# Input tiles of SyncE's queue wait for weight loads of GpSimd's queue

## The chip, the cores and the metric

The kernel runs on the eight cores of one Trainium2 chip, one program on all of them. Each core has five engines that run their own instruction streams: TensorE (PE, with its weight loads as PEld), VectorE (DVE), ScalarE (ACT), GpSimd (POOL) and SyncE (SP). Sixteen DMA engines move data between the memory of the chip and the core's own memory. Here two engines issue DMAs: SyncE asks for input tiles and writes the output (queue q1 of the profile), GpSimd asks for weights, which are float32 in memory and bfloat16 on arrival (queue q0). The metric is the device time in microseconds of the slowest core; less is better.

## The reference, cut to what matters

One layer of a decoder trunk over x of (4, 4096, 1024):

```python
h = rmsnorm(x, norm_mix)
proj = h @ w_in                       # 4608 columns: u_pool, u_rnn, u_gate, two merge gates
y_pool = pool_mixer(u_pool, w_pool_grp, pool_scale) @ w_pool_out   # causal means over 2/4/8/16
v = causal_depthwise_conv(u_rnn, conv_w, conv_b)                   # width 4
hr = rg_lru(v, ...)                   # h_t = a_t h_{t-1} + b_t, a sequential scan over time
y_rnn = (hr * gelu(u_gate)) @ w_rnn_out
x = x + (g_merge[0] * y_pool + g_merge[1] * y_rnn) @ w_o
h = rmsnorm(x, norm_ffn)
x = x + (silu(h @ w_ffn_gate) * (h @ w_ffn_up)) @ w_ffn_out        # inner width 2816
return rmsnorm(x, norm_final)
```

## The kernel before

Each of the four sequences is shared by two cores. An even core (role a) computes the first 2240 positions, an odd core (role b) the rest. Role b has no state from its neighbour: it first runs a shortened pass over the first 2240 positions in five tiles ("prefix") to get the scan's state, and then its own positions. Both roles are in one program; behind a common head each engine loads the role (L1242) and branches (L1246).

All data are held transposed, channels on partitions and time along the free axis, in tiles of 256 to 512 columns. An input tile of w columns is four buffers `xt` of two channel blocks each, and one DMA per buffer (`load_tile`). For the first norm ScalarE squares a buffer (L623), GpSimd adds the squares up (L638, L640) or TensorE sums them directly, TensorE sums over partitions (L667), ScalarE makes the reciprocal root (L671, L674), and VectorE makes `h` (L682). TensorE then runs the projections, eight matmuls for each weight tile and column tile (L705). In the recurrent branch a group of eight matmuls `bank<-h,wu` is followed by the convolution (ScalarE L745, VectorE L757), a cast to `vb` (L765, on GpSimd), two gate matmuls (L770) and their tanh (L780).

Nothing of the order is written by hand. `Graph` records the operations with their buffers; `Planner.run` places them on the five engines by keys and a cost model, in which one DMA follows the other at `dma_rate` (185,000 bytes per us) with `dma_lat` (2.2 us) behind; `place` and `reuse` give the buffers addresses. Only then `signals` turns dependences into semaphore waits. Each engine executes its list in order, so whatever waits holds up all that stands behind it. Every operation has a planned `start` and `end`. For a DMA, `end` is the planned landing.

Besides true dependences `signals` adds one kind of wait on purpose: a weight load on GpSimd, outside the head, waits for the last input tile whose planned landing is not after the load's planned start. Input tiles wait for no weight.

The head (the same in both roles) asks for the first tile of 260 columns and the constants on SyncE, and on GpSimd for `wu` (the first of four), `keep_rg` and the other three `wu`. Behind the branch role b's SyncE asks for sixteen buffers in a row, those of prefix tiles two to five, and role a's for eight, those of its tiles two and three. GpSimd goes on with weights, five in role b and some twenty in role a before it runs dry.

Of the kernel before, what the change touches and what calls it, by code (L numbers as in the profile page):

```python
# [142 lines left out]
class Planner:  # L143
# [273 lines left out]
    def signals(self, dma_count):  # L417

        seq = sorted(self.g.ops, key=lambda o: (o.start, o.idx))
        pos = {}  # L420
        for e in ENGINES:
            for i, o in enumerate(self.order[e]):
                pos[o.idx] = i
        chan_last = {}
        for e in ("sp", "pool"):
            n = 0
            for o in self.order[e]:
                if not o.nbytes:
                    continue
                c = (e, n % DMA_SEMS[e])  # L430
                o.sem = c
                o.val = 16 * (n // DMA_SEMS[e] + 1)
                p = chan_last.get(c)
                if p is not None:
                    o.deps.append(p)
                chan_last[c] = o
                n += 1

        tiles = sorted([o for o in self.order["sp"] if o.nbytes and o.tag != "out"], key=lambda o: o.end)
        for o in self.order["pool"][sum(h.eng == "pool" for h in self.head):]:  # L440
            if o.nbytes:
                t = [x for x in tiles if x.end <= o.start]
                if t:
                    o.deps.append(t[-1])
        for o in self.head:
            o.sig = not o.nbytes
        for o in seq:
            for d in o.deps:
                if d.nbytes or d.eng != o.eng or o.eng != "pe":
                    d.sig = True  # L450
        for e in ENGINES:
            v = 0
            for o in self.order[e]:
                if o.nbytes:
                    continue
                if o.sig:
                    v += 1
                    o.sem = e
                    o.val = v
        know = {e: {} for e in ENGINES}  # L460
        self.waits = {}
        for o in seq:
            k = know[o.eng]
            need = {}
            for d in sorted(o.deps, key=lambda d: -d.start):
                if not d.nbytes and d.eng == o.eng == "pe":
                    continue
                if k.get(d.sem, 0) >= d.val or need.get(d.sem, (0,))[0] >= d.val:
                    continue
                need[d.sem] = (d.val, d)  # L470
            out = []
            for s, (v, d) in sorted(need.items(), key=lambda x: -x[1][1].end):
                if k.get(s, 0) >= v:
                    continue
                out.append((s, v))
                k[s] = v
                for ks, kv in d.know.items():
                    if k.get(ks, 0) < kv:
                        k[ks] = kv
            self.waits[o.idx] = out  # L480
            o.know = dict(k)
            if o.sem is not None:
                o.know[o.sem] = max(o.know.get(o.sem, 0), o.val)
        self.chan_last = chan_last
# [11 lines left out]
class Role:  # L496
# [464 lines left out]
    def chunk(self, ci, widths, kk, pre, wus, col):  # L961
# [153 lines left out]
        begin=dict(pe=6.0, act=4.0, dve=3.0, pool=9.0, sp=9.5), window=72.67, table_pen=78.88, dma_rate=185000.0, dma_lat=2.2,  # L1115
# [17 lines left out]
        begin=dict(pe=14.0, act=9.0, dve=11.5, pool=15.0, sp=10.0), window=94.49, table_pen=12.12, dma_rate=185000.0,  # L1133
        dma_lat=2.2, lag=0.08, pe_lag=0.5, bank_lag=0.05, lead=16.65, xlead=8.05, reserve=16380.0, near=29.3, cap=191092.0,
# [198 lines left out]
```

How the kernel before makes its waits and increments, by code:

```python
        def emit(e, name, pl, lo=0, hi=None):  # L1225
            for o in pl.order[name][lo:hi]:
                for s, v in pl.waits[o.idx]:
                    e.wait_ge(sems[s], v)
                ins = o.fn(e)
                if o.nbytes:
                    ins.then_inc(sems[o.sem], 16)
                elif o.sig:
                    ins.then_inc(sems[name], 1)
            if name == "sp" and hi is None:
                for o in pl.role.out_ops:
                    e.wait_ge(sems[o.sem], o.val)
```

## Time and profile before

| | before |
|---|---|
| median of 3 runs (lowest to highest) | 1023.6 us (1023.18 to 1025.88) |
| the profiled execution's own time | 1024.35 us |
| its longest span (core 3, role b) | 1022.8 us |
| its shortest span (core 2, role a) | 1016.8 us |
| TensorE busy, core 3 | 924.4 us (90%) |
| VectorE, ScalarE, GpSimd busy | 591.4, 556.7, 336.8 us |
| wait of TensorE on DMA wu | 11.0 us, in two pieces |

A span runs from the first to the last instruction of one core. The time is about that of the longest span with what lies around it, here 1.55 us in the profiled execution. The profile is of one execution; all cores' traces were read. The engines' busy times are shares of the same span and overlap; an idle engine costs time only where another waits for it.

### The profile page before, as it was taken

The page shows a single profiled execution, that of the slowest core. Times are in us where ns is not written, and L with a number is a line of the kernel's source. Part 1 is how long each engine was busy: PE and PEld are TensorE (multiplying, and loading weights), DVE is VectorE, ACT ScalarE, POOL GpSimd, SP SyncE. Part 2 cuts the span into 40 slices and gives each one's busy share as a digit, 9 for nine tenths or more (in the row PEclk, how much of TensorE's full clock was granted, in tenths as well). Part 3 has the DMA queues.
Part 4 walks back from the last instruction along what each step waited for, and adds up shares of the span by engine and source line. Part 5 has one row for each costly group of instructions (what it writes and reads, how often), then busy time and mean ns, then how long its engine had stood idle before and what let it go on. Part 6 is the DMA issues. An engine that isn't in the chain of part 4 may idle for free.

```text
span 1022.8 us, 13708 instructions; the slowest of 8 cores (1016.8 to 1022.8 us)
## 1 busy us (share of the span) xinstructions
PE 924.4 (90%) x4484; PEld 446.6 (44%) x4484; DVE 591.4 (58%) x798; ACT 556.7 (54%) x804; POOL 336.8 (33%) x347
## 2 busy tenths in 40 slices
PE   2378688698978999999999999999999999999995
PEld 1134233233433444444444444444555555555553
DVE  2179998999999867844253544533644452222235
ACT  2579997989889942548264938611722351111112
POOL 2438593778655641151001122112251211000000
PEclk8579789899989999999999999999999999999998
DMA  8921452003644276768403257255939175910003
GB/s 176 242 69 33 160 93 42 12 1 55 116 82 87 38 192 118 160 98 150 82 8 56 39 80 141 44 101 123 253 69 212 30 129 108 211 41 2 1 1 135
DMA packets 42765, 96.88 MB, mean 95 GB/s; under 512 B 3776, under 2 KB 19264, under 8 KB 42560
## 3 DMA queue, kind: packets, MB, share of 16 engines
q0 software_dynamic: 23904, 63.45, 36.1%
q1 hardware_dynamic: 18784, 32.48, 10.6%
q8 instruction: 40, 0.66, 0.2%
q14 instruction: 37, 0.30, 0.1%
HBM read 151.75 MB, written 7.60 MB: 156 GB/s over the span
## 4 chain that ended last, share of the span: by engine, by line
PE 78%; ACT 9%; issue 5%; POOL 3%; DVE 2%; DMA 2%; ACTq 0%; DVEq 0%; SPq 0%; POOLq 0%
PE bank L705 74%; PE bank L770 2%; PE bank L667 2%; DMA wu<-w_in 2%; ACT th L780 1%; DVE v L757 1%; ACT q L798 1%; POOL sq L638 1%; ACT th L788 1%; ACT v L745 1%; ACT L798 1%; ACT L780 1%; DMA xt<-xT 1%; POOL vb L765 1%; ACT wi L780 0%
## 5 line engine op out<-in xcount | busy, mean ns | idle before, releaser
L705 PE MATMUL bank<-h,wf 128*128 128x508 bf16 (+2 forms) x1408 | 280.7, 358 | 0.0
L705 PEld LDWEIGHTS bank<-h,wf 128*128 128x128 bf16 x1408 | 136.5, 97 | 139.9 <-issue 0.8
L757 DVE SCALAR_TENSOR_TENSOR v<-bank,keep_cst,v 128x496 f32<-128x496 f32 (+3 forms) x200 | 128.8, 683 | 32.4 <-POOL v L754 13.4
L705 PE MATMUL bank<-h,wu 128*128 128x500 bf16 (+4 forms) x576 | 130.1, 381 | 16.3 <-DMA wu<-w_in 11.0
L1084 DVE TENSOR_TENSOR ff<-tf,bank 128x508 bf16<-128x508 f32 (+2 forms) x88 | 55.7, 634 | 147.9 <-PE bank L705 123.5
L705 PE MATMUL bank<-ff,wz 128*128 128x508 bf16 (+2 forms) x704 | 139.5, 359 | 0.0
L1079 ACT ACTIVATE tf<-bank 128x508 f32<-128x508 f32 (+2 forms) x88 | 48.8, 557 | 137.8 <-PE bank L705 134.4
L652 ACT ACTIVATE sq<-x 128x508 f32<-128x508 f32 (+2 forms) x56 | 32.9, 590 | 125.3 <-DVE x L1096 97.4
L705 PEld LDWEIGHTS bank<-ff,wz 128*128 128x128 bf16 x704 | 68.9, 98 | 68.6 <-issue 0.5
L705 PEld LDWEIGHTS bank<-h,wu 128*128 128x128 bf16 x576 | 58.7, 103 | 83.9 <-issue 32.9
L765 POOL CAST vb<-v 128x496 bf16<-128x496 f32 (+3 forms) x68 | 61.1, 905 | 61.4 <-DVE v L757 53.3
L770 PE MATMUL bank<-vb,keep_rg 128*128 128x496 bf16 (+4 forms) x144 | 43.2, 381 | 33.4 <-ACT th L780 10.1
L515 POOL DMA_DIRECT2D wf<-wfi x44 | 23.8, 549 | 147.1 <-PE bank L705 106.0
L795 POOL TENSOR_TENSOR q<-th 128x752 f32<-128x752 f32 (+3 forms) x31 | 56.9, 1843 | 37.8 <-ACT th L788 18.9
L682 DVE SCALAR_TENSOR_TENSOR h<-xt,keep_cst,bank 128x500 bf16<-128x500 f32 (+4 forms) x72 | 45.8, 686 | 30.8 <-ACT bank L674 29.7
L745 ACT ACTIVATE v<-bank,keep_cst 128x496 f32<-128x496 f32 (+3 forms) x72 | 51.7, 732 | 19.1 <-PE bank L705 18.0
L705 PE MATMUL bank<-h,wa 128*128 128x508 bf16 (+2 forms) x256 | 56.6, 367 | 3.0 <-ACT th L780 1.7
L1096 DVE TENSOR_TENSOR x<-bank,x 128x508 f32<-128x508 f32 (+2 forms) x32 | 20.4, 639 | 64.9 <-PE bank L705 64.6
L705 PE MATMUL bank<-h,wg 128*128 128x508 bf16 (+2 forms) x256 | 55.2, 367 | 2.8 <-ACT th L780 1.9
L780 ACT ACTIVATE th<-bank,keep_hb 128x496 f32<-128x496 f32 (+3 forms) x72 | 44.8, 639 | 22.1 <-PE bank L770 21.8
L638 POOL TENSOR_TENSOR sq<-sq,sq 128x1000 f32<-128x1000 f32 (+2 forms) x18 | 41.9, 2330 | 36.9 <-ACT sq L623 30.3
L705 PE MATMUL bank<-h,wb 128*128 128x508 bf16 (+2 forms) x256 | 53.9, 363 | 0.0
(103 smaller groups left out, 1311.7 us busy)
## 6 DMA issues: line engine op xcount, KB each, us to landing
wf<-wfi POOLq DMA_DIRECT2D x44, 512.0 KB, 9.5
wz<-wfo POOLq DMA_DIRECT2D x16, 704.0 KB, 10.1
xt<-xT SPq DMA_DIRECT2D x16, 500.0 KB, 8.6
wu<-w_in POOLq DMA_DIRECT2D x16, 256.0 KB, 13.7
xt<-xT SPq DMA_DIRECT2D x8, 512.0 KB, 21.1
wa<-w_in POOLq DMA_DIRECT2D x16, 256.0 KB, 5.9
wg<-w_in POOLq DMA_DIRECT2D x16, 256.0 KB, 5.4
wb<-w_in POOLq DMA_DIRECT2D x16, 256.0 KB, 5.5
```

Of the source, the lines that this page charges most:

```text
L638: self.ew(adds, 2 * w, key, lambda e, t=t: e.tensor_tensor(out=sq.tensor[:], in0=sq.tensor[:], in1=t.tensor[:], op=ALU.add), [sq, t], [sq] ...
L652: g.op("act", c_act(w), key, lambda e: e.activation(out=s.tensor[:], in_=x2[cc // 2].tensor[:, cc % 2, :], func=AF.Square), rd=[(x2[cc // ...
L682: g.op("dve", c_dve(w) + 0.04, key + 0.1 * kc, lambda e, kc=kc, b=b, o=o, h=h: e.scalar_tensor_tensor(out=o.tensor[:, h, :], in0=b.tensor[ ...
L705: last = e.matmul(p.tensor[:, 0:n], lhsT=wap(kc), rhs=rhs(kc), start=(kc == 0), stop=(kc == K - 1))
L745: g.op("act", c_act(w, 2), k, lambda e, p=p, o=o, w=w: e.activation(out=v.tensor[:, o:o + w], in_=p.tensor[:, HALO:HALO + w], func=AF.Iden ...
L757: g.op("dve", c_dve(w), k, lambda e, p=p, o=o, w=w, s=s: e.scalar_tensor_tensor(out=v.tensor[:, o:o + w], in0=p.tensor[:, HALO - s:HALO - ...
L765: cast = lambda e, vb=vb, o=o, w=w: e.tensor_copy(out=vb.tensor[:], in_=v.tensor[:, o:o + w])
L770: g.op("pe", c_mm(w) + 0.05, k + 1 + 0.3 * q, lambda e, pg=pg, q=q, vb=vb, w=w: e.matmul(pg.tensor[:, 0:w], lhsT=self.rg.tensor[:, q, j, : ...
L780: g.op("act", c_act(w, 1), k + 1 + 0.3 * q, lambda e, pg=pg, out=out, hcol=hcol, w=w: e.activation(out=out(), in_=pg.tensor[:, 0:w], func= ...
L795: g.op("pool", 0.09 + 0.0018 * W, k, lambda e: e.tensor_tensor(out=q2.tensor[:], in0=th.tensor[:], in1=th.tensor[:], op=ALU.mult), rd=allp ...
L1079: g.op("act", c_act(w), kf, lambda e, pg=pg, th=th, w=w: e.activation(out=th.tensor[:], in_=pg.tensor[:, 0:w], func=AF.Silu), rd=[pg], wr= ...
L1084: g.op("dve", c_dve(w), kf, lambda e, pu=pu, th=th, fb=fb, w=w: e.tensor_tensor(out=fb.tensor[:], in0=th.tensor[:], in1=pu.tensor[:, 0:w], ...
```

## The change

In `signals`, behind the rule for weight loads, a second rule looks the other way. For each input load of SyncE outside the head it takes the time at which the plan lets its transfer begin (planned landing less latency less size over rate). Of the weight loads on GpSimd that the plan has landed by then, and that the plan starts before this load, the last to land becomes a dependence. Nothing is planned anew: orders, buffers and addresses stay, only waits are added, and a few that they cover fall away.

```diff
         for o in self.order["pool"][sum(h.eng == "pool" for h in self.head):]:
             if o.nbytes:
                 t = [x for x in tiles if x.end <= o.start]
+                if t:
+                    o.deps.append(t[-1])
+
+        weights = sorted([o for o in self.order["pool"] if o.nbytes], key=lambda o: o.end)
+        for o in self.order["sp"][sum(h.eng == "sp" for h in self.head):]:
+            if o.nbytes and o.tag != "out":
+                begin = o.end - self.prm["dma_lat"] - o.nbytes / self.prm["dma_rate"]
+                t = [x for x in weights if x.end <= begin and x.start < o.start]
                 if t:
                     o.deps.append(t[-1])
```

In the lists of instructions a wait on `d_pool2` is one for the landing of GpSimd's third DMA (they are counted from 0): d_pool0 is the first `wu`, d_pool1 `keep_rg`, d_pool2 to d_pool4 the other three `wu`, d_pool5 the first weight behind the branch. `s_dve`, `s_pe` and `s_act` are waits for an engine's results. SyncE of role a, from its branch on, before:

```order
L1246 COMPARE_AND_BRANCH
L515 DMA xt_70<-xT 128x2x416
L515 DMA xt_71<-xT 128x2x416
L515 DMA xt_72<-xT 128x2x416
L515 DMA xt_73<-xT 128x2x416
L515 DMA xt_83<-xT 128x2x400
L515 DMA xt_84<-xT 128x2x400
L515 DMA xt_85<-xT 128x2x400
L515 DMA xt_86<-xT 128x2x400
```

The same place of the changed kernel:

```order
L1254 COMPARE_AND_BRANCH
L523 DMA xt_70<-xT 128x2x416 [waits d_pool2]
L523 DMA xt_71<-xT 128x2x416 [waits d_pool3]
L523 DMA xt_72<-xT 128x2x416 [waits d_pool4]
L523 DMA xt_73<-xT 128x2x416
L523 DMA xt_83<-xT 128x2x400
L523 DMA xt_84<-xT 128x2x400
L523 DMA xt_85<-xT 128x2x400
L523 DMA xt_86<-xT 128x2x400 [waits d_pool5]
```

No load has moved; the first three of the second tile, and the last of the third, have a wait each. SyncE of role b, the first six of its sixteen prefix loads, before:

```order
L515 DMA xt_1034<-xT 128x2x500
L515 DMA xt_1035<-xT 128x2x500
L515 DMA xt_1036<-xT 128x2x500
L515 DMA xt_1037<-xT 128x2x500
L515 DMA xt_1076<-xT 128x2x500
L515 DMA xt_1077<-xT 128x2x500
```

The same place of the changed kernel:

```order
L523 DMA xt_1034<-xT 128x2x500 [waits d_pool3]
L523 DMA xt_1035<-xT 128x2x500 [waits d_pool4]
L523 DMA xt_1036<-xT 128x2x500
L523 DMA xt_1037<-xT 128x2x500
L523 DMA xt_1076<-xT 128x2x500
L523 DMA xt_1077<-xT 128x2x500
```

The first two have a wait for the third and the fourth `wu`; they and the fourteen behind them stand in the same order. SyncE of role b where its own first tiles are asked for, behind the sixteen of the prefix, before:

```order
L515 DMA xt_1048<-xT 128x2x500 [waits s_pe]
L515 DMA xt_1049<-xT 128x2x500 [waits s_pe]
L515 DMA xt_1050<-xT 128x2x500
L515 DMA xt_1051<-xT 128x2x500 [waits s_dve]
L515 DMA xt_1062<-xT 128x2x500
L515 DMA xt_1063<-xT 128x2x500 [waits s_dve]
L515 DMA xt_1064<-xT 128x2x500 [waits s_pe]
L515 DMA xt_1065<-xT 128x2x500
```

The same place of the changed kernel, where d_pool10 is a `wq` and d_pool11 the `wa` behind it:

```order
L523 DMA xt_1048<-xT 128x2x500 [waits d_pool10]
L523 DMA xt_1049<-xT 128x2x500 [waits d_pool11,s_pe]
L523 DMA xt_1050<-xT 128x2x500
L523 DMA xt_1051<-xT 128x2x500
L523 DMA xt_1062<-xT 128x2x500
L523 DMA xt_1063<-xT 128x2x500 [waits s_dve]
L523 DMA xt_1064<-xT 128x2x500 [waits s_pe]
L523 DMA xt_1065<-xT 128x2x500
```

The first two have a weight to wait for, and two waits on engines are covered by it.

## Rows read from the trace of the kernel before

**Rows 1.** Spans of the cores: core, span, mean granted TensorE clock.

```profile
core 2: 1016.8 us, clock 0.986
core 3: 1022.8 us, clock 0.951
core 6: 1021.7 us, clock 0.985
```

**Rows 2.** Timeline, core 3, TensorE: start, length in us, instruction, count, [idle before, releaser].

```profile
19.44 1.89 PE L705 MATMUL bank<-h,wu 128*128 128x260 bf16 x8 [6.16 <-DMA wu<-w_in]
26.14 1.89 PE L705 MATMUL bank<-h,wu 128*128 128x260 bf16 x8 [4.80 <-DMA wu<-w_in]
...
31.57 1.94 PE L705 MATMUL bank<-h,wu 128*128 128x260 bf16 x8
...
60.99 7.63 PE L705 MATMUL bank<-h,wu 128*128 128x500 bf16 x32
```

**Rows 3.** Chain of work, core 3, 0 to 62 us: start, length in us, what.

```profile
8.48 0.67 POOL wu L563
...
9.67 16.34 DMA wu<-w_in
```

**Rows 4.** Timeline, core 3, ScalarE.

```profile
37.87 2.88 ACT L623 ACTIVATE sq<-xt 128x1000 f32<-128x1000 f32 x3
```

**Rows 5.** DMA queues from 24 to 36 us, core 2, then core 3: packets, MB, share.

```profile
q0 software_dynamic: 789, 1.43, 71.0%
q1 hardware_dynamic: 758, 1.14, 34.4%
...
q0 software_dynamic: 694, 1.26, 62.4%
q1 hardware_dynamic: 691, 1.30, 39.1%
```

**Rows 6.** DMA queues from 44 to 54 us, core 2, then core 3.

```profile
q0 software_dynamic: 961, 1.75, 109.3%
...
q1 hardware_dynamic: 1502, 2.90, 98.8%
```

**Rows 7.** Single DMAs, core 3, at 341, 97.7, 7.0 us: KB, us to landing.

```profile
wo<-wo POOLq DMA_DIRECT2D x1, 256.0 KB, 4.0
...
xt<-xT SPq DMA_DIRECT2D x1, 500.0 KB, 4.0
...
xt<-xT SPq DMA_DIRECT2D x1, 500.0 KB, 7.3
```

**Rows 8.** Timeline, core 3, VectorE.

```profile
14.50 3.25 DVE L682 SCALAR_TENSOR_TENSOR h<-xt,keep_cst,bank 128x260 bf16<-128x260 f32 x8 [2.69 <-ACT bank L674]
```

**Rows 9.** Timeline, core 3, GpSimd.

```profile
20.98 2.12 POOL L515 DMA_DIRECT2D wu<-w_in  x4 [9.71 <-issue]
...
25.18 0.40 POOL L765 CAST vb<-v 128x256 bf16<-128x256 f32 x1 [1.56 <-DVE keep_hs L591]
30.64 0.40 POOL L765 CAST vb<-v 128x256 bf16<-128x256 f32 x1 [5.07 <-DVE v L757]
```

**Rows 10.** Timeline, GpSimd's first weight behind the branch, core 2, then core 6.

```profile
14.52 0.53 POOL L515 DMA_DIRECT2D wq<-w_in  x1 [3.30 <-issue]
...
21.36 0.53 POOL L515 DMA_DIRECT2D wq<-w_in  x1 [10.35 <-issue]
```

**Rows 11.** Timeline, core 2, ScalarE.

```profile
43.07 0.86 ACT L623 ACTIVATE sq<-xt 128x800 f32<-128x800 f32 x1
```

**Rows 12.** Single DMA, core 3, at 103.6 us.

```profile
wa<-w_in POOLq DMA_DIRECT2D x1, 256.0 KB, 6.9
```

**Rows 13.** Timeline, core 3, ScalarE, later.

```profile
122.85 6.58 ACT L623 ACTIVATE sq<-xt 128x1000 f32<-128x1000 f32 x7
```

**Rows 14.** Single DMAs, core 2, at 712.5 and 719.9 us.

```profile
x<-xT SPq DMA_DIRECT2D x1, 332.0 KB, 11.7
...
x<-xT SPq DMA_DIRECT2D x1, 332.0 KB, 26.1
```

## The prediction, made before the changed kernel ran

> **What bounds the kernel now.** I read the spans of the cores first. Time is the slowest core, and there are two programs: the odd cores run role b and end at 1022.8 us, the even cores run role a, of which core 2 needs 1016.8 us and core 6 1021.7 us [rows 1]. So a gain must come in role b, and beyond about 1 us in core 6, beyond 6 us in all of role a. The profiled execution took 1024.35 us, 1.55 more than its longest span; the median of the runs, 1023.6, is 0.8 above that span, and I add 0.8 to spans.
>
> The page's busy times come second: TensorE is busy for 90% (the table above), so what can be won is its idle time. The one DMA that it is said to wait for is the weight tile wu, in the first 27 us: the timeline of core 3 shows an idle of 6.16 us before the first projection group and of 4.80 us before the second, both ended by wu [rows 2]. The chain of work says how far that reaches: 16.34 us stand on a wu in flight (issued 9.67, landed 26.0), then come four projection groups one after the other, then the squares of the second input tile (three of them from 37.87 on), GpSimd's additions with their sum acc, and only behind it the burst of 32 matmuls at 60.99 [rows 2 to 4]. The whole start of role b hangs on a weight landing.
>
> Why do the weights land so late? In the stretch from 24 to 36 us both DMA queues are full. On core 3 the weights' queue (q0) moves 1.26 MB in 12 us, 105 GB/s, and the input tiles' queue (q1) 1.30 MB, 108 GB/s; on core 2 they move 119 and 95 [rows 5]. Alone, from 44 to 54 us, q0 reaches 175 GB/s on core 2 and q1 290 on core 3 [rows 6]. Meanwhile the tiles that share the engines are not wanted yet: the one asked for at 6.99 is there 7.3 us later [rows 7], and ScalarE squares most of the second tile from 37.87 on [rows 4].
>
> **The change, part by part.** Only SyncE's order gains waits, 24 in role a's program and 17 in role b's; no instruction moves. Nearly all of the effect is at the start, where SyncE now stands before the second input tile until a weight has landed.
>
> *Weights.* The first wu is issued at 8.48 [rows 3]. A weight of this size that is alone lands after 4.0 us [rows 7], so at 12.5. Behind it in the queue a weight of 262,144 B takes 1.5 us at 175 GB/s and keep_rg, twice that, 3.0: keep_rg lands at 15.5, the second wu at 17.0, the third at 18.5, the fourth at 20.0. The second landed at 26.0 before, so 9 us are gained there.
>
> *Role b, compute.* What is late next is h of the first tile: VectorE makes it from 14.50 on for 3.25 us [rows 8], so group 1 starts at 17.9 instead of 19.44 and group 2 at 19.8 instead of 26.14. Not all of these 6.3 us arrive. GpSimd is past its branch only at 20.98 and issues five weights of some 0.53 us before its first cast [rows 9], so that cast can start at 23.6 instead of 25.18, and the two gate matmuls behind it at 24.1. Group 3 stands after them: 24.7. The second cast follows its group by 4.5 us as before (30.64 behind 26.14), and the constants that VectorE still owes add 1: 25.3. Its gate matmuls wait for group 3 until 26.4, and group 4 starts at 27.0 instead of 31.57: 4.6 us earlier. From there to the burst every step is a compute step as long as before, if the tiles are there.
>
> *Role b, tiles.* xt of tile two is asked for at 18.5 and 20.0; a tile that is alone lands after 4.0 us [rows 7], so the first at 22.5. Then five weights (issued from 20.98 on) share the engines: 5 x 2.5 us, from 22 to 34.5. At 108 GB/s a tile of 512,000 B takes 4.7 us: the second lands at 27.2, the third at 31.9, and the fourth, finished at 290 GB/s, at 35.3; the next tiles follow every 1.8 us. Shifted by 4.6, the last three squares of this tile stand at 33.3, 34.2 and 35.1 [rows 4]. The fourth buffer is 0.2 us late, so role b keeps 4.4 us: 1018.4.
>
> *Role a.* It pays. Its second tile waits from 6.7 until 17.0, and its GpSimd issues its next weight at 14.52 [rows 10] and then some twenty more, so q0 never empties and every tile goes at the shared 95 GB/s: 4.5 us for 425,984 B, 4.3 for 409,600. The sixth of them is the one that hurts: its square stands in ScalarE's order before the exponential that VectorE's h waits for. Four tiles at 4.5 and two at 4.3 make 26.6 us. If transfer begins 1 us after the ask, it lands at 44.6; if I charge the 2.2 us by which a lone tile exceeds its 1.8 us at full rate, at 45.8. Its square was at 43.07 [rows 11]: 1.5 to 2.7 us late, I take 2.0. The last two tiles of the eight follow at the same pace. The weights' gain is no help here, because the tile comes last. Core 2 goes to 1018.8.
>
> *The rest of the program.* I cost it at nothing. Role b's first own tile is the next place: eight tiles from 97.7 on (the first landed after 4.0 us [rows 7]) wait for a wq and a wa, and the wa lands only at 110.5 [rows 12]. Behind the waiting SyncE stand only the other tiles. The second then lands at 114.5 and the last at 125.3, 1.8 us apart; ScalarE squares the first seven from 122.85 to 129.43 [rows 13] and the last after that, so 4 us of cover are left, and what the start gains moves both sides alike. If that cover were gone, each us would go straight to ScalarE. In role a's last chunk the tiles asked for around 712 and 720 us land 11.7 and 26.1 us later [rows 14], in order in one ring; the new waits end before the transfer ahead does, so they move nothing. TensorE's own waits for six or seven weights fall away with SyncE's; they were met long before.
>
> The sum: the slowest core is then role a's at 1018.8, with role b at 1018.4, and the time 1018.8 + 0.8 = 1019.6 us.
>
> **Rivals.** *A late role load in one role-a core.* GpSimd's idle before its first weight of the role is 3.30 us on core 2 and 10.35 us on core 6, and that alone makes core 6 end 4.9 us later [rows 1, 10]. If one even core still meets this, it ends at 1021.7 whatever role b does: 1022.5 us. For it: one of four cores did. Against: the load falls in 10 to 18 us, when fewer transfers run now. 20%.
>
> *Role a's tiles come somewhat later still.* Each 0.3 us of pace costs 1.8 us at the sixth tile; at 4.9 us a tile it is 4.3 to 5.5 us late, the time 1021.9 to 1023.1. 14%.
>
> *Slower: role a starves.* If weights take more than their half, as around 712 to 746 us, where four tiles landed between 724.2 and 746.0, 7.3 us apart [rows 14], the sixth tile lands at 17 + 2.2 + 6 x 7.3 = 63, 20 us late, less the few that ScalarE could give: 1037. It decides against the old kernel from about 5.5 us a tile on. Against it: there the weights have twice the size, and from 24 to 36 us, beside weights of the size that matters, the share was 95 GB/s. 8%.
>
> *It brings nothing.* That the waits are met when SyncE reaches them is excluded at the start: it asks at 7 us, and no weight lands before 12.5. But late tiles could give role b's 4.4 us back: 1023.6. For it: eight or sixteen tiles stand behind the first wait. Against it: SyncE has no other work there, and q1 alone empties its sixteen tiles at 1.8 us each. 8%.
>
> A rule that speaks for this rival stands on the Trainium skill's page "DMA: Bandwidth & Descriptors", in "Rules for kernel authors": overlap DMA with compute by issuing early and waiting late. By that rule holding tiles back brings nothing, and the time would stay at 1023.6. The trace speaks against it at this one place, where TensorE waits 11.0 us for weights and nobody yet for the tiles beside them.
>
> **How the numbers follow.** The forecast, 50%, is 1019.6 and runs from 1017.6 (role b gains the full 6.3 us and role a loses nothing) to 1020.5. Some 0.3%, 3.1 us, is what a measurement of this kernel can tell from no change, so 1020.5 is the border of faster. The late load, the mildly late tiles and no effect make "same" 42%, starvation makes "slower" 8%. A range to 1022.9 leaves out only the last two rivals and a little of the low side: 1017.4 to 1022.9.
>
> **What would show it.** In the new profile: the two idles on wu (6.16 and 4.80 us) gone or under 2 us, the second group near 20 and the burst of 32 near 56.5 on core 3; GpSimd's acc about 4.5 us earlier; on core 2 the square of the sixth tile at 44.5 to 46 with a wait on xt. Odd cores near 1018.4, even cores at 1018 to 1019.5. Wrong would be: role b's squares waiting for xt, an even core with 10 us idle before its first role weight, or a new wait of ScalarE on xt near 122 us.

## The result and the profile after

The changed kernel is slower: 1029.92 us (median of 7 runs) against 1023.6, a ratio of 1.0056 with a 95% interval of 1.0043 to 1.0069. The forecast was 1019.6 with a range to 1022.9, so it missed on the wrong side. The ratios, and the medians of even and odd cores, leave out executions in which a whole die ran at a lower clock. The profiled execution took 1029.35 us, 1.55 more than its longest span.

Spans of the cores after the change, as [rows 1]: core, span, mean granted TensorE clock.

```profile
core 2: 1026.1 us, clock 0.983
core 3: 1020.7 us, clock 0.957
core 6: 1027.8 us, clock 0.978
core 7: 1017.1 us, clock 0.957
```

The odd cores (role b) gained a little, the even cores (role a) lost, and the slowest core is now an even one. The medians of the even cores went from 1018.4 to 1026.0 us, those of the odd cores from 1021.7 to 1020.7 (before: 19 runs on the chip of the first four experiments below; after: 6 runs).

What was bought is there. The timeline of TensorE on core 3 after the change, as [rows 2] (start, length, instruction, [idle before, releaser]):

```profile
17.09 1.33 PE L713 MATMUL bank<-h,wu 128*128 128x260 bf16 x8 [4.72 <-DVE h L690]
19.41 1.46 PE L713 MATMUL bank<-h,wu 128*128 128x260 bf16 x6 [0.98 <-DMA wu<-w_in]
22.46 0.59 PE L713 MATMUL bank<-h,wu 128*128 128x260 bf16 x2 [1.59 <-issue]
...
27.31 1.94 PE L713 MATMUL bank<-h,wu 128*128 128x260 bf16 x8
...
29.47 1.94 PE L713 MATMUL bank<-h,wu 128*128 128x260 bf16 x8
...
62.38 3.97 PE L713 MATMUL bank<-h,wu 128*128 128x500 bf16 x18
```

The idle on `wu` before the first group is gone (6.16 us before) and the one before the second is 0.98 us (4.80 before); the second group starts at 19.41 instead of 26.14 (its last two matmuls follow only at 22.46, behind an idle of 1.59 us for which the profile shows no wait). But the fourth group has kept only 2.1 us of that, and the burst, at 62.38, comes 1.4 us later than before. (This core's span is shorter all the same, by 2.1 us, and not through the start: at 150 us it is still 0.1 us behind the old trace and at 155 us 1.5 us ahead, and in this stretch its granted clock was 1.00, the level of 2.4 GHz, where it had been 0.55, near that of 1.2; TensorE had been busy for 7.4 and 7.5 of the 10 us ahead. Core 7, whose tiles came earlier, is 5.6 us ahead from 50 us on and 5.1 us at the end.)

What was paid shows in the chain of work of core 6, from 0 to 80 us (start, length, what):

```profile
10.77 12.31 DMA wu<-w_in
...
23.09 0.02 SPq L1236
...
24.97 28.73 DMA xt<-xT
...
53.79 0.04 ACT sq L631
...
55.23 4.01 DVE h L690 x7
```

Here the new wait can be read as one chain: a head weight lands at 23.07, SyncE (SPq) is released by it, issues the loads that stood behind that wait, the sixth of role a's eight (the second of its third tile) at 24.97, and that load stays 28.7 us in flight. ScalarE squares it at 53.79 and `h` follows. Before, the chain of this stretch knew no `xt` behind the first tile. ScalarE on core 2 says the same; the last row answers to [rows 11]:

```profile
42.94 0.90 ACT L631 ACTIVATE sq<-xt 128x832 f32<-128x832 f32 x1 [2.45 <-DMA xt<-xT]
47.70 0.87 ACT L631 ACTIVATE sq<-xt 128x800 f32<-128x800 f32 x1 [3.86 <-DMA xt<-xT]
51.94 0.87 ACT L631 ACTIVATE sq<-xt 128x800 f32<-128x800 f32 x1 [1.45 <-DMA xt<-xT]
```

The square of the sixth load is at 51.94 instead of 43.07, 8.9 us late, and every step behind it on core 2 is 8 to 11 us late up to the end (1026.1 against 1016.8). Behind 60 us the shift no longer grows.

The two DMA queues of core 2, from 20 to 24 us and then from 24 to 36 us (packets, MB, share of 16 engines), show why:

```profile
q0 software_dynamic: 414, 0.75, 108.7%
q1 hardware_dynamic: 2, 0.00, 0.3%
...
q0 software_dynamic: 739, 1.34, 68.7%
q1 hardware_dynamic: 730, 1.16, 36.3%
```

SyncE asks at 20.08, but until 24 us the weights' queue q0 has the engines for itself; only 2 packets of q1 start. From then on both queues start nearly the same number of packets, as in [rows 5]. GpSimd's first weight behind its branch stands at 18.09 on core 2 and at 23.62 on core 3, as [rows 9, 10]:

```profile
18.09 0.54 POOL L523 DMA_DIRECT2D wq<-w_in  x1 [6.81 <-issue]
...
23.62 2.12 POOL L523 DMA_DIRECT2D wu<-w_in  x4 [12.19 <-PE bank L713]
```

On core 2 that is before SyncE's ask: four weights of the role stand in q0 by then, behind two of the head.

### The profile page after: what moved, and what is told of

Read it like the earlier page. It is cut to its first block, busy times and chain, and to the rows that moved or that the text cites. A ratio compares the mean times of both kernels' runs of the same rounds, so it can differ in the third digit from the quotient of the medians.

```text
span 1027.8 us, 16823 instructions; the slowest of 8 cores (1017.1 to 1027.8 us)
## 1 busy us (share of the span) xinstructions
PE 983.7 (96%) x6038; PEld 599.4 (58%) x6038; DVE 526.5 (51%) x813; ACT 446.8 (43%) x750; POOL 214.5 (21%) x280
## 4 chain that ended last, share of the span: by engine, by line
PE 91%; DMA 5%; DVE 2%; issue 1%; ACT 1%; SPq 0%; POOL 0%; DVEq 0%; POOLq 0%; ACTq 0%
PE bank L713 88%; DMA xt<-xT 3%; PE bank L778 1%; PE bank L675 1%; DMA wu<-w_in 1%; DVE v L765 1%; DVE h L690 0%; DVE x L690 0%; SPq L523 0%; DVE wi L836 0%; PE bank L615 0%; ACT v L753 0%; DVE gl L846 0%; POOL wu L571 0%; ACT bank L682 0%
## 5 line engine op out<-in xcount | busy, mean ns | idle before, releaser
L713 PE MATMUL bank<-h,wf 128*128 128x396 bf16 (+5 forms) x2112 | 339.8, 321 | 0.0
L713 PEld LDWEIGHTS bank<-h,wf 128*128 128x128 bf16 x2112 | 205.1, 97 | 131.7 <-issue 1.9
L1092 DVE TENSOR_TENSOR ff<-tf,bank 128x344 bf16<-128x344 f32 (+5 forms) x132 | 70.4, 542 | 194.1 <-PE bank L713 158.6
L713 PE MATMUL bank<-ff,wz 128*128 128x256 bf16 (+5 forms) x1056 | 169.8, 321 | 0.0
L765 DVE SCALAR_TENSOR_TENSOR v<-bank,keep_cst,v 128x500 f32<-128x500 f32 (+5 forms) x144 | 81.6, 599 | 27.3 <-ACT v L753 22.1
L713 PE MATMUL bank<-h,wu 128*128 128x400 bf16 (+5 forms) x384 | 69.5, 334 | 6.7 <-DVE sp L597 4.7
L713 PE MATMUL bank<-h,wb 128*128 128x256 bf16 (+5 forms) x384 | 65.1, 321 | 0.0
L713 PE MATMUL bank<-h,wg 128*128 128x256 bf16 (+5 forms) x384 | 64.3, 321 | 0.2 <-DVE v L765 0.2
L713 PE MATMUL bank<-h,wa 128*128 128x256 bf16 (+5 forms) x384 | 64.5, 321 | 0.0
L713 PE MATMUL bank<-gl,wr 128*128 128x256 bf16 (+5 forms) x384 | 63.8, 321 | 0.0
```

The lines of the kernel that those rows point to most:

```text
L713: last = e.matmul(p.tensor[:, 0:n], lhsT=wap(kc), rhs=rhs(kc), start=(kc == 0), stop=(kc == K - 1))
L765: g.op("dve", c_dve(w), k, lambda e, p=p, o=o, w=w, s=s: e.scalar_tensor_tensor(out=v.tensor[:, o:o + w], in0=p.tensor[:, HALO - s:HALO - ...
L1092: g.op("dve", c_dve(w), kf, lambda e, pu=pu, th=th, fb=fb, w=w: e.tensor_tensor(out=fb.tensor[:], in0=th.tensor[:], in1=pu.tensor[:, 0:w], ...
```

## The experiments

Theory: the loss is made in role a before 60 us, because the second tile is asked for behind a queue that is already filled with weights, and more of them follow. Rivals: the 35 waits behind the start; cores that hinder each other; the late ask alone, whatever is queued. Times are compared with runs of the kernel before on the same chip. The diffs are cut to the lines that matter and touch the planner, not the arithmetic; they are against the changed kernel, or against the kernel with the weights moved where the text says so.

### Which waits, and in which role

```diff
 # in the loop over SyncE's loads, one of three conditions
-            if o.nbytes and o.tag != "out":
+            if o.nbytes and o.tag != "out" and o.start >= 80:                               # e1
+            if o.nbytes and o.tag != "out" and o.start < 80 and self.prm["prefix"]:         # e2, role b
+            if o.nbytes and o.tag != "out" and o.start < 80 and not self.prm["prefix"]:     # e3, role a
```

> Only the waits of loads planned behind 80 us are kept (20 in role a, 15 in role b); the start is as in the kernel before. Theory 'start': the loss is made in the first 60 us and carried to the end one for one, so this kernel gives 1023.6 us, within 1.5, and role a's sixth tile of the second input tile lands near 33 us as before. Rival 'later waits': the many waits behind the start hold loads back; then 1027 to 1030 us, and a compute step behind 80 us waits for a load that it did not wait for before.

> Only role b's two waits at the start are kept; role a and everything later as before. Theory 'start, role a pays': even cores return to their 1017 to 1022 us, odd cores keep what they gained (1015 to 1022), so the time is 1020 to 1023 us. Rival 'coupled cores': the even cores lose because the odd cores' weights now load at the same time as theirs; then even cores stay above 1024 and the time at 1026 to 1030.

> Only role a's four waits at the start are kept. Theory 'start, role a pays': even cores 1023 to 1029 us as in the changed kernel, odd cores 1022.7 as before, time 1028 to 1031. Rival 'coupled cores' (role a's loss needs role b's change too): even cores at most 1022, time 1022 to 1024.

| | ratio to before | 95% interval | median of even cores | of odd cores |
|---|---|---|---|---|
| before, same chip | 1 | | 1018.4 us | 1021.7 us |
| only later waits | 1.0001 | 0.9991 to 1.0010 | 1018.3 | 1021.8 |
| only role b's start waits | 0.9980 | 0.9971 to 0.9989 | 1018.1 | 1019.2 |
| only role a's start waits | 1.0035 | 1.0022 to 1.0048 | 1025.7 | 1021.0 |

The later waits do nothing that can be measured. The even cores lose 7.3 us by role a's four waits alone, and lose nothing by role b's two, which make the odd cores 2.5 us faster. So half of the change, in role b, is a small gain. Much more could not come of it alone, because the slowest even core ends as late as before (1020.1 us in the median, 1020.5 before; the slowest odd core 1020.8, 1023.3 before).

Whether role b's waits cost role a something on top was left open, since the whole change had 1.0056 in another set of runs; both were run side by side.

> The changed kernel itself on the same chip as the next run, to see whether role b's waits cost role a anything. Theory 'role a alone': the same time as with role a's waits only, 1.0035 of the kernel before, within 0.0015, so 1027.5 to 1029.5 us; even cores end no later than there. Rival 'role b adds to it': 1.005 to 1.007 again, 1029.5 to 1031 us, and the slowest even core ends 1 to 3 us later than with role a's waits only.

> Only role a's four start waits, beside the changed kernel on one chip. Theory 'role a alone': 1027.5 to 1029.5 us and equal to the changed kernel within 1.5 us. Rival 'role b adds to it': 1.5 to 2.5 us faster than the changed kernel.

The changed kernel took 1.0050 (1.0035 to 1.0064), role a's waits alone 1.0039 (1.0025 to 1.0053): 0.8 us between the medians, with even cores at 1026.1 and 1025.7. By its bound of 1.5 us the theory holds; by the other, 1029.5 us, the changed kernel lies on the border with 1029.52. A cost of up to a us or so can't be excluded.

### Late ask or filled queue

The next kernel keeps the change's rule and takes the weights away from in front of the tiles. Behind `run`, GpSimd's weights of the role are moved in its list behind the casts they stood among. Their new planned start also makes the old rule (a weight waits for the tile planned to land before it) tie role a's to the fourth load of the second tile; on cores 2 and 6 of its trace that wait was met when GpSimd reached it. And one of role a's four start waits falls away, that of the eighth load for the first weight behind the branch, which now starts later; the three that set the ask stay.

```diff
+    def hold(self, idx, start):
+        pool = self.order["pool"]
+        n = sum(h.eng == "pool" for h in self.head)
+        at = [o.idx for o in pool].index(idx) + 1
+        moved = [o for o in pool[n:at] if o.nbytes]
+        self.order["pool"] = pool[:n] + [o for o in pool[n:at] if not o.nbytes] + moved + pool[at:]
+        for i, o in enumerate(moved):
+            o.start = start + 0.01 * i
...
+HOLD = dict(a=(296, 37.2), b=(123, 54.9))     # behind role a's fourth cast, behind role b's third sum
...
+    if role in HOLD:
+        pl.hold(*HOLD[role])
     pl.signals(None)
```

> The changed kernel with all its waits, and GpSimd's own-role weights moved: in role a the 26 weights stand behind the fourth cast and wait for the fourth load of the second input tile, in role b the 5 weights stand behind the sum of the third input tile. Theory 'backlog': role a's tiles are late because a dozen weights already stand in the other queue when the first of them is asked for; with that queue empty the first tile lands 4 to 6 us behind its ask (12.5 us in core 6 of the changed kernel), the sixth before 36 us (53.7 there), even cores end at 1012 to 1017, odd cores at 1013 to 1020, time 1016 to 1020. Rival 'late ask': the tile is late because it is asked for at 20 and not at 7 us, whatever else is queued; then the first tile still lands near 30, the sixth behind 43, and even cores stay above 1022. A second rival, 'weights late': the weights held back are missed by TensorE before 80 us; then even cores end above 1020 with TensorE waiting for a weight between 40 and 80 us.

Measured: 1019.11 us, a ratio of 0.9942 (0.9928 to 0.9956): 0.6% faster than the kernel before. Even cores have a median of 1014.4 us, odd cores of 1015.7. Its spans:

```profile
core 2: 1015.7 us, clock 0.987
core 3: 1015.6 us, clock 0.958
core 6: 1013.8 us, clock 0.989
```

The ask is as late as in the changed kernel (19.1 and 19.3 us on cores 2 and 6, there 20.1 and 20.7). The first load on core 6, asked for at 20.7 in the changed kernel and at 19.3 here (KB, us to landing; the first row is of the changed kernel):

```profile
xt<-xT SPq DMA_DIRECT2D x1, 416.0 KB, 12.5
```

```profile
xt<-xT SPq DMA_DIRECT2D x1, 416.0 KB, 4.4
```

So the ask's lateness is not what delays the tile. From 24 to 34 us core 2 now moves tiles almost alone, and ScalarE finds the fifth and the sixth load there (queues first, then ScalarE's timeline):

```profile
q1 hardware_dynamic: 1683, 2.56, 93.9%
q0 software_dynamic: 18, 0.04, 4.2%
...
39.23 0.87 ACT L641 ACTIVATE sq<-xt 128x800 f32<-128x800 f32 x1 [0.50 <-PE bank L685]
42.41 0.86 ACT L641 ACTIVATE sq<-xt 128x800 f32<-128x800 f32 x1
```

The sixth load lands at 33.1 us (51.9 in the changed kernel) and waits 9 us to be squared: the releaser of the square ahead of it is TensorE. Role b's burst moves as well, to where the forecast had put it (56.5):

```profile
56.76 6.94 PE L723 MATMUL bank<-h,wu 128*128 128x500 bf16 x32
```

And the weights that came later are not missed: the first of them lands at 37.2 us on core 2 and is used at 44.8, and on none of the cores does TensorE wait for a DMA from 30 to 80 us. The rival 'weights late' falls with that.

Is the moved order alone the gain? The same kernel without any of the change's waits:

```diff
-            if o.nbytes and o.tag != "out":
+            if o.nbytes and o.tag != "out" and False:
```

> The weights moved as in the run before (26 behind role a's casts, 5 behind role b's third tile sum), but none of the change's waits: SyncE asks for the second tile at 7 us as in the kernel before. Theory 'the waits are worth something once the queue is empty': the first four wu share the engines with the tiles again and land at 19 to 30 us as before (12.3 to 22.3 with the waits), role b's second group stands near 26 instead of 19.5, odd cores end at 1019 to 1022, time 1021 to 1024. Rival 'it was the order of the weights alone': odd and even cores end as with the waits, 1014 to 1017, time 1018 to 1019.5.

0.9994 (0.9984 to 1.0004), even cores 1017.8, odd cores 1021.8. Asked for at 7 us, the tiles again share the engines with the head's weights, and core 3 has its two idles of [rows 2] back:

```profile
19.14 1.89 PE L723 MATMUL bank<-h,wu 128*128 128x260 bf16 x8 [6.52 <-DMA wu<-w_in]
25.96 1.89 PE L723 MATMUL bank<-h,wu 128*128 128x260 bf16 x8 [4.93 <-DMA wu<-w_in]
```

So the 0.6% needs both halves: the moved weights alone bring nothing and the waits alone cost 0.5% (of them, role b's two alone bring 0.2%). The waits let the head's weights land early, and the moved weights keep that from being paid back by the tiles.

### How much queue is too much

Two graded runs. In the first, four of role a's 26 weights stay in front of the casts; in the second nothing is moved and role a's start loads wait for the first `wu` only, 6 us earlier.

```diff
 # e6: hold, with four weights of role a left where they were
+        stay = 0 if self.prm["prefix"] else 4
+        moved = [o for o in pool[n:at] if o.nbytes][stay:]
+        self.order["pool"] = pool[:n] + [o for o in pool[n:at] if o not in moved] + moved + pool[at:]
```

```diff
 # e7: without hold
                 t = [x for x in weights if x.end <= begin and x.start < o.start]
+                if o.start < 80 and not self.prm["prefix"]:
+                    t = t[:1]
```

> Waits and moved weights, but in role a the first four of the 26 weights stay where the kernel before has them. Theory 'backlog at the ask': with some weights queued when the first tile is asked for, its first packets come 2 to 4 us behind the ask and it lands 7 to 10 us behind it (4.3 to 4.7 with all 26 moved, 8.9 and 12.5 with none); when these four have landed, near 32 us, the tiles run alone, so the sixth lands at 36 to 40 us (33 with all moved, 52 to 54 with none). Even cores end within 3 us of those with all 26 moved. Rival 'it is the steady issue of GpSimd, not the queue': the first tile lands within 5 us of the ask as with all moved.

> The changed kernel, but in role a the four loads at the start wait for the first wu only (landed at 14.1 to 14.3 us there; the second at 20.6). No weight moved. Theory 'backlog': asked for near 14 us, behind the four head weights and beside the role's weights, each tile goes at the shared pace of 4.1 to 4.6 us; the sixth lands at 42 to 46 us and even cores end at 1017 to 1023; odd cores as in the changed kernel, 1015 to 1024; time 1020 to 1024. Rival 'late ask': the sixth tile comes 6.5 us earlier than in the changed kernel, 45.5 to 47, and even cores end at 1019 to 1023; the two part only by the first tile: within 6 us of its ask by 'late ask', 8 us and more by 'backlog'.

With four weights left (0.9948, 0.9933 to 0.9964; even cores 1014.3) the first load lands 9.1 to 10.6 us behind its ask, as bad as in the changed kernel, though GpSimd issues no weight beyond these four before it has landed (on core 0 all four stand ahead of the ask, on core 2 one); the sixth lands at 37.8 to 40.6, which ScalarE and TensorE still hide. With the early ask (0.9998, 0.9988 to 1.0009; even cores 1021.8) the first load takes some 11 us on all four even cores:

```profile
xt<-xT SPq DMA_DIRECT2D x1, 416.0 KB, 11.2
```

It was asked for at 13.3 us on core 2, behind `keep_rg` and three `wu` of the head, and from 13 to 18 us only q0 moves:

```profile
q0 software_dynamic: 259, 0.66, 103.9%
```

By the mark set beforehand (within 6 us of the ask, or 8 and more) this is 'backlog'. The sixth load came at 47.3 to 48.7 us, later than either theory had it, and hardly earlier than on cores 0 and 4 of the changed kernel (48.0 and 48.7), which had asked 3 to 4 us later: what was won at the ask was lost behind the queue.

Put together over these kernels, from the packet records and the landings (weights outstanding: issued before the ask and not yet landed at it; the loads of the kernel before are single ones from later in the program, asked for when no other load of SyncE was in flight):

| kernel, core | ask at | weights outstanding | first packet of q1 behind the ask | first load landed behind the ask |
|---|---|---|---|---|
| before, 3 (500 KB) | 97.7 us | 0 | 1.0 us | 4.0 us |
| before, 2 (412 KB) | 171.1 | 0 | 1.0 | 3.6 |
| before, 2 (412 KB) | 185.6 | 7 | 3.7 | 9.0 |
| before, 3 (508 KB) | 302.4 | 1 | 3.6 | 6.9 |
| after, 3 | 21.1 | 1 | 1.0 | 5.3 |
| all weights moved, 6 | 19.3 | 2 | 1.3 | 4.4 |
| all weights moved, 2 | 19.1 | 2 | 2.1 | 4.3 |
| only role a's start waits, 6 | 19.0 | 2 | 1.6 | 8.5 |
| only role a's start waits, 4 | 18.8 | 2 | 1.7 | 9.0 |
| all but four moved, 2 | 19.9 | 3 | 2.4 | 10.6 |
| after, 0 | 16.9 | 3 | 2.6 | 8.8 |
| asked behind the first wu, 2 | 13.3 | 4 (one is keep_rg) | 4.9 | 11.2 |
| after, 4 | 16.5 | 5 | 4.4 | 9.6 |
| all but four moved, 0 | 19.6 | 6 | 3.7 | 10.2 |
| after, 2 | 20.1 | 6 | 3.9 | 8.9 |
| after, 6 | 20.7 | 6 | 3.5 | 12.5 |

The first packet mostly waits longer the more weights are queued, 1.0 us with none and 3.5 to 4.9 with four to seven, and not for all of them: on core 6 after the change it starts at 24.2, when two of the six have landed. The count isn't a rule: with a single weight outstanding the first packet came 3.6 us behind the ask at 302.4 us, where that weight had been issued 0.65 us ahead, and 1.0 us behind it at 21.1 us, where the weight landed 1.2 us later; and at a few other places of the trace of before a load with nothing outstanding waited up to 2.4 us. What makes an engine take the other queue at that point, and not before, none of these runs shows. The landing hangs on more than the first packet: with two weights outstanding the first load came 4.3 to 4.4 us behind its ask where no weight followed, and 8.5 to 9.0 us where GpSimd went on issuing. So weights that follow the ask delay the load too.

### Role b alone, and the best version without later waits

```diff
-HOLD = dict(a=(296, 37.2), b=(123, 54.9))
+HOLD = dict(a=(296, 37.2))                  # e8
```

> The changed kernel with the weights moved in role a only; role b has its five weights ahead of the first cast. Theory: even cores 1012 to 1017 us as with both moved; odd cores as in the changed kernel, 1015 to 1024, since there the fourth tile lands near 44 us instead of 33 and the first cast stands behind five weight issues; time 1020 to 1024. Rival 'role b does not need it': odd cores at 1014 to 1018 and the time at 1018 to 1019.5.

0.9967 (0.9951 to 0.9983): even cores 1013.7, odd cores 1017.1 with up to 1021.9. Role b seems to need the move too, though the interval overlaps those of the runs with role b's weights moved: on the same chip the slowest odd core ends at 1020.8 us in the median, and at 1018.3 with all but four moved. ScalarE on core 1 still waits for tiles, where core 3 of the kernel with both moved doesn't wait for one up to the sixth square (the row is of core 1 here).

```profile
40.62 1.04 ACT L641 ACTIVATE sq<-xt 128x1000 f32<-128x1000 f32 x1 [3.21 <-DMA xt<-xT]
```

Last, both moved, with the change's waits for loads planned before 80 us only (the condition `o.start < 80`):

> Both roles' weights moved and the change's waits kept only for the loads planned before 80 us (four in role a, of which three are left, two in role b). Theory: the later waits do nothing, so it gives what the kernel with all waits and moved weights gave, 0.994 of the kernel before, 1018 to 1020 us. Rival: some later wait helps or harms once the start is faster; then it differs from 0.994 by over 0.002.

1020.66 us, 0.9959 (0.9947 to 0.9972). By the expectation's bound of 0.002 it is the same as with all waits (0.9942), but the odd cores' medians are 2.3 us apart (1018.0 and 1015.7) in two sets of runs whose runs of the kernel before differ by 0.7 us there (1021.0 and 1021.7), so it isn't settled whether role b's later waits help there.

## Why the prediction was wrong

**What bounds the kernel: right.** The two idles on `wu` were the price of the tiles beside them; without the tiles the second group came at 19.41 (forecast 19.8), and role b's gain of 4.4 us was there as soon as nothing else stood in the way (burst at 56.76, odd cores down 6.0 us in the median).

**Weights alone: right on two of four even cores.** The second `wu` was put at 17.0. It landed at 16.5 and 16.8 on cores 4 and 0, but at 20.0 and 20.6 on cores 2 and 6. The 175 GB/s of the step came from a stretch, 44 to 54 us, in which the queue ran alone; on core 6 from 14 to 20 us, where it ran alone too but all eight cores load the same weights, it moved 133 GB/s; that the other cores are the cause isn't shown (the row below is of the changed kernel: stretch, length, busy us of PE, PEld, DVE, ACT and POOL, granted clock, DMA share, GB/s).

```profile
14.00:20.00 6.00, 1.58 (x8) 0.89 (x8) 3.65 (x11) 2.17 (x5) 1.00 (x2) 0.80 1.03 133
```

**Role a's tiles: here the prediction failed.** The step read "If transfer begins 1 us after the ask, it lands at 44.6; if I charge the 2.2 us by which a lone tile exceeds its 1.8 us at full rate, at 45.8." The pace behind it was right, the beginning was not:

| | forecast | core 0 | core 4 | core 2 | core 6 |
|---|---|---|---|---|---|
| ask | 17.0 us | 16.9 | 16.5 | 20.1 | 20.7 |
| first packet, behind the ask | 1 us | 2.6 | 4.4 | 3.9 | 3.5 |
| first load, behind the ask | 5.5 to 6.7 us | 8.8 | 9.6 | 8.9 | 12.5 |
| each of the next five | 4.4 us | 4.5 | 4.5 | 4.6 | 4.1 |
| sixth load lands | 44.6 to 45.8 | 48.0 | 48.7 | 51.9 | 53.7 |

On cores 0 and 4 the ask came when forecast and the whole excess, 2 to 4 us, is the first load; on cores 2 and 6 the ask adds 3 to 4 us. I had taken a lone load's begin and end for those of one behind a filled queue: alone (at 97.7 us) the first packet comes 1.0 us behind the ask, and of the other 3.0 us until it lands 1.2 are more than the 1.8 at full rate. Behind the weights the first packet alone took 2.6 to 4.4 us. From it to the landing it was 6.2, 5.3, 5.0 and 9.0 us on cores 0, 4, 2 and 6, where the step had 4.5 to 5.7. So on three cores the wait for the first packet is all or most of the excess over the upper bound, 6.7 us; why core 6 took 9.0 us stays open. The errors of ask and begin have one sign. The price per us was right: on every even core the shift at the sixth square is within 2 us of the shift at the end. The even cores' median went up by 7.6 us where 2.0 was forecast.

The sum also started too low. Core 2 with 1016.8, the fastest core of one execution, was taken for role a; the median of even cores is 1018.4, and that of the slowest even core of an execution, which bounds the time, 1020.5. With the step's own 2.0 us on top, the time would have been 1022.5 + 0.8 = 1023.3: no gain even by the forecast's own price.

The Trainium skill's page "DMA: Bandwidth & Descriptors" says in "Queues, rings and completion order" that each DMA engine takes turns between the queues it has work for, packet by packet. The trace agrees once both run (739 and 730 packets in 12 us). In the 4 us behind the ask there are 414 packets to 2. Whether the load had work on the engines by then the trace doesn't show, so it doesn't tell whether the rule fails there; but the measurement decides what a load costs, and a sum that lets it take its turns from a lone load's begin on puts it too early.

**Role b's compute and tiles: half right.** GpSimd's first weight behind the branch came at 23.62, not at 20.98, so its first cast was late (26.22, forecast 23.6) and the fourth group gained 2.1 us instead of 4.6. And its five weights and the tiles then shared the engines until 45 us: the fourth load landed at 44.2 us on core 3 (33.6 on core 7, forecast 35.3). ScalarE's wait for it is what pushed the burst to 62.38:

```profile
44.33 1.04 ACT L631 ACTIVATE sq<-xt 128x1000 f32<-128x1000 f32 x1 [6.20 <-DMA xt<-xT]
```

**The rest of the program at nothing: right.** The later waits alone gave 1.0001.

**Rivals.** The slower case was named with its mechanism, late tiles in role a, and given 8%. But it was tied to a pace above 5.5 us a tile, and the pace stayed at 4.1 to 4.6; "tiles somewhat later" was priced by pace as well. No case priced the time to the first packet. At the start of the kernel before there was nothing to read it from, for the tiles were asked for at 6.7 us with no weight issued yet. But later in the same trace it stood: on core 2 a load of 412 KB, nearly the size of role a's tiles, landed 9.0 us behind its ask at 185.6 us with seven weights outstanding, and 3.6 us behind it at 171.1 with none; on the other even cores the first of these landed 8.3 to 9.7 us behind its ask. The two single DMAs of core 2 before (KB, us to landing):

```profile
x<-xT SPq DMA_DIRECT2D x1, 412.0 KB, 9.0
...
x<-xT SPq DMA_DIRECT2D x1, 412.0 KB, 3.6
```

Read from there, the first load would have been put at some 9 us instead of 5.5 to 6.7, as it was on three of the four cores. "It brings nothing" by the rule to issue early and wait late (the Trainium skill's page "DMA: Bandwidth & Descriptors", "Rules for kernel authors") came nearer to the outcome than the forecast, and yet the rule isn't the whole: with the queue cleared, waiting gives 0.6%, and without the waits that gain is gone (0.9994).

## What to carry to other kernels

Holding one stream of transfers back to let another land early pays only if the engines are free when the held stream is asked for; ask what the other queue has issued by that moment and issues behind it, and move that too. Price the first transfer behind a filled queue apart from the pace of those that follow, from a place in the trace where a load was asked for in that state; a lone transfer says nothing about it. Where two kinds of core do the same work in different order, make the sum for each, from its slowest core over several executions, since one of them pays for what the other gains.

## What the runs showed of the hardware

- A load asked for on SyncE's queue had its first packet 1.0 us behind the ask when it was alone (in a few places up to 2.4), 1.3 to 2.1 us with two weights of 256 KB outstanding on the other queue, and 2.4 to 4.9 us with three to seven (the table above; with one it was 1.0 or 3.6 us), although once both run the two queues start nearly the same number of packets (739 and 730 in 12 us).
- The weights' queue, alone on its core, moved 133 GB/s from 14 to 20 us on core 6 of the changed kernel, when all eight cores load the same weights, and 175 from 44 to 54 us on core 2 before [rows 6].
- GpSimd's idle ahead of its first weight of the role, 3.30 and 10.35 us on cores 2 and 6 before [rows 10] and 9.71 on core 3 [rows 9], was 5.1 to 7.7 us on the four even cores after the change and 12.19 us on core 3. So it isn't a fixed cost; what sets it, the runs don't show.
